# Three input products on unnormalised tiles instead of two, with the first taken out of its bank ahead of the norm's tiles

## The reference, cut to what matters

```python
def rmsnorm(x, g):
    xf = x.astype(jnp.float32)
    y = xf * lax.rsqrt(jnp.mean(xf * xf, axis=-1, keepdims=True) + NORM_EPS)
    return (y * g.astype(jnp.float32)).astype(x.dtype)

for i in range(DEPTH):                      # DEPTH = 2
    h = rmsnorm(x, norm_mix[i])
    proj = h @ w_in[i]
    q, k, v, cb, cc, cx, u, g = jnp.split(proj, IN_SPLITS, axis=-1)
    ...                                     # attention, convolution, state-space scan of u, gates
    x = x + merged @ w_mix_o[i]
    ...                                     # feed-forward
```

## Time and profile before

| | |
|---|---|
| median of three runs | 2523.43 us |
| lowest and highest | 2518.66, 2524.77 us |
| profiled execution | 2524.5 us, of which its span 2522.6 us |

### The profile page before, as it was taken

One profiled execution on the slowest core, in us unless ns is written; L12 is line 12 of the kernel. 1 busy time (PEld: TensorE's weight loads), 2 busy tenths in 40 slices (PEclk: granted clock), 3 DMA queues, 4 the chain that ended last, 5 costly groups with the idle time before them and its releaser, 6 DMA issues.

```text
span 2522.6 us, 33251 instructions
## 1 busy us (share of the span) xinstructions
PE 2433.3 (96%) x12455; PEld 1950.5 (77%) x12455; DVE 1231.0 (49%) x2254; ACT 929.1 (37%) x1470; POOL 1223.1 (48%) x1590
## 2 busy tenths in 40 slices
PE   7899999999999999999999999998988998999999
PEld 5778777888888778877788878887665677788887
DVE  6884653452335668356333143254678844511211
ACT  5233442432322532244242232243436654423322
POOL 3443445555556645354555555564333432555554
PEclk9999999999999999999999999999999999999999
DMA  4222222332222232222233223232310011223232
GB/s 158 85 81 74 91 67 92 108 105 98 96 97 92 93 101 79 82 84 72 88 101 123 96 90 100 88 105 70 115 61 9 1 42 34 100 93 101 93 100 92
DMA packets 81151, 218.06 MB, mean 86 GB/s; under 512 B 15840, under 2 KB 25440, under 8 KB 80608
## 3 DMA queue, kind: packets, MB, share of 16 engines
q1 hardware_dynamic: 61776, 200.43, 24.4%
q10 hardware_dynamic: 19216, 15.51, 2.2%
HBM read 207.26 MB, written 2.10 MB: 83 GB/s over the span
## 4 chain that ended last, share of the span: by engine, by line
PE 84%; DVE 11%; issue 2%; ACT 2%; ACTq 1%; POOL 1%; DMA 0%; DVEq 0%
PE psG L1010 25%; PE psG L1012 25%; PE psG L1011 25%; DVE work_b L2068 1%; PE psT L1189 1%; PE psS L1166 1%; PE psO L1222 1%; DVE tmp L2068 1%; DVE work_m L2068 1%; DVE work_b L2398 1%; PE psS L1097 1%; DVE work_b L2533 1%; ACTq L1717 1%; DVE max L2532 1%; DVE small_work L2068 1%
## 5 line engine op out<-in xcount | busy, mean ns | idle before, releaser
L949 POOL TENSOR_TENSOR w_lo<-w_raw,w_hi 128x256 fp32r<-128x256 f32 x1478 | 1152.0, 810 | 1187.4 <-ACT w_hi L1586 1187.3
L1010 PE MATMUL psG<-h_hi,w_hi 128*128 128x512 f32 x1872 | 747.4, 399 | 12.3 <-POOL w_lo L949 4.1
L1011 PE MATMUL psG<-h_lo,w_hi 128*128 128x512 f32 x1872 | 734.0, 392 | 0.0
L1012 PE MATMUL psG<-h_hi,w_lo 128*128 128x512 f32 x1872 | 733.9, 392 | 0.0
L1586 ACT ACTIVATE w_hi<-w_raw 128x1024 fp32r<-128x1024 f32 (+3 forms) x416 | 402.9, 969 | 501.5 <-PE psG L1012 486.4
L1010 PEld LDWEIGHTS psG<-h_hi,w_hi 128*128 128x128 f32 x1872 | 354.8, 190 | 102.2 <-issue 18.8
L1012 PEld LDWEIGHTS psG<-h_hi,w_lo 128*128 128x128 f32 x1872 | 354.4, 189 | 75.3
L1011 PEld LDWEIGHTS psG<-h_lo,w_hi 128*128 128x128 f32 x1872 | 355.1, 190 | 72.4 <-issue 1.7
L1010 PE MATMUL psG<-m_hi,w_hi 128*128 128x512 f32 x800 | 311.8, 390 | 1.1 <-DVE m_lo L2068 1.1
L1012 PE MATMUL psG<-m_hi,w_lo 128*128 128x512 f32 x800 | 311.4, 389 | 0.0
L1011 PE MATMUL psG<-m_lo,w_hi 128*128 128x512 f32 x800 | 311.4, 389 | 0.0
(11 more groups left out here) (374 smaller groups left out, 2617.4 us busy)
## 6 DMA issues: line engine op xcount, KB each, us to landing
w_raw<-wstream SPq DMA_DIRECT2D x326, 512.0 KB, 3.3
w_raw<-wstream SPq DMA_DIRECT2D x64, 256.0 KB, 2.6
w_raw<-wstream SPq DMA_DIRECT2D x16, 384.0 KB, 3.0
work_b<-work_b ACTq DMA_DIRECT2D x16, 256.0 KB, 3.7
work_b<-cmpw ACTq DMA_DIRECT2D x2, 2048.0 KB, 8.6
x<-xT SPq DMA_DIRECT2D x4, 512.0 KB, 7.1
small_work<-ssmp ACTq DMA_DIRECT2D x8, 256.0 KB, 2.8
outT<-x SPq DMA_DIRECT2D x8, 256.0 KB, 2.0
```

What stands on the lines that cost most here:

```text
L949: ins = pool.tensor_tensor(lo[:, c], w[:, c], hi[:, c].bitcast(F32), ALU.subtract)
L1010: pe.matmul(out, whi, hi, start=(k == 0), stop=False)
L1011: pe.matmul(out, whi, lo, start=False, stop=False)
L1012: ins = pe.matmul(out, wlo, hi, start=False, stop=(k == K - 1))
```

## The change

UNSCALED becomes 3: u0, u1 and u2 run on the tiles without the factor, u3 is the first that reads the norm's. By the same constant, the mean of squares and the spread in layer 0 stand in u2 instead of u1, and `s_read` is counted by u2. VectorE takes u0 out of its bank inside normalise, once the factor is there and ahead of the tiles, since u3 needs this bank; u1 and u2 follow after the tiles. u2 is multiplied out by VectorE and no longer copied by ScalarE.

```diff
-UNSCALED = 2
+UNSCALED = 3
...
                 if name in late:
                     dve.wait_ge(s_rs, late_no[name] + 1)
+                    take_mixer(first_job[name])
                 base = h_norm[name]
...
                 normalise(f"mix{l}", ("norm_mix", l))
-                for i in range(UNSCALED):
+                for i in range(1, UNSCALED):
                     take_mixer(("u", l, i))
```

## The result

| | before | changed |
|---|---|---|
| median, runs on the same chips | 2522.01 us (16 runs, 2517.93 to 2524.77) | 2526.34 us (16 runs, 2521.28 to 2529.22) |
| profiled execution, its span | 2524.5, 2522.6 us | 2527.99, 2526.1 us |

The ratio is 1.0018, 95% interval 1.0011 to 1.0025: 4.3 to 4.5 us slower, between 2.8 and 6.3. That is less than the 0.3% that the prediction took for the least a measurement can tell from no change; the interval is narrower than that and excludes no change. The predicted difference was + 7.4: the time lies in the range and the sign is right, the size is too large.

A forecast was written before the change was run, and what follows sets the result against it. VectorE, not the busy TensorE, was taken to set layer 0's time until 89 us. Layer 0's + 7.7 and layer 1's - 0.3 sum to + 7.4 us, giving 2530.8 us, range 2524.5 to 2535.0.

The forecast's parts named there:

- The mean of squares moves back: Layer 0's norm: the mean moves from u1 to u2, the spread starts 5.4 us late, the norm's tiles 6.1 late.
- Nothing bought on TensorE, q0 waits for its weights: Layer 0: u3 ends at about 46.2 as before; q0 waits for its weights' low part until 48.1, losing 2 us.
- VectorE behind the tiles: Layer 0: u1 and u2 are multiplied out after the tiles, then the coefficients follow, 6.1 us late, at 47.3.
- Contention with GpSimd: Layer 0: GpSimd's weight splits slow 4 more of VectorE's small operations by some 0.5 us each, + 1.9 us.
- The sines absorb nothing: Layer 0: VectorE's 3.01 us pause lies beside ScalarE's sines, so only a 0.4 us margin absorbs delay.
- 7.7 us late is what reaches 88.96 and all that follows: Layer 0's VectorE delay of 7.7 us reaches the scan's first products at 88.96 and everything after in full.
- Rival A: The forecast itself, from + 5.5 us (no added GpSimd contention) to about + 9.5; chance 0.62.
- rival B: VectorE's delay is absorbed; only TensorE's 2.1 us at q0's weights stay: + 1.8 us, 2525.2; chance 0.15.
- Layer 1: Root not delayed; u3's wait for a tile disappears, last tile at about 878.7, a gain of 0.3 us.
- Rival C: TensorE's half-rate clock after its wait ahead of q3 costs 3.6 us; uncovered + 11.0, 2534.4; chance 0.13.
- Rival D: The extra product fills TensorE's wait in layer 0 and the root isn't late: about - 3 us, 2520.4; chance 0.05.
- The last test that the prediction proposed: Prediction is wrong if the distance from 88.96 to the end of the span changes by more than 2 us.

The follow-up runs named there:

- the first experiments: Against the kernel before: the change in layer 0 only, 2527.79 us; the changed kernel with VectorE's scan angles computed before the root, 2527.25 us.
- layer 0 alone: Three unscaled products in layer 0, two in the other layer as in the kernel before: 2527.79 us, ratio 1.0034 against the kernel before.
- in three parts on three products: Changed kernel with the mean of squares in u1 and two thirds of VectorE's scan angles in two earlier pauses: 2520.11 us, ratio 0.9992 against the kernel before.
- the angles ahead of the root: Changed kernel with VectorE computing layer 0's scan angles before the reciprocal, while waiting for the late root: 2527.25 us, ratio 1.0030 against the kernel before.

## Why the prediction was right or wrong, point by point

- **The mean of squares moves back** (predicted: mean at 30.1, reciprocal at 31.4, spread at 33.1, first tile at 35.7): 30.10, 31.48, 33.08, 35.65. Right to 0.1 us, and shown by the kernel that puts it back (27.74, 30.43, no loss).
- **Nothing bought on TensorE, q0 waits for its weights** (u3 from 37.9 to 46.2, q0 at 48.1): 37.94, 46.3 (last start 46.04 + 0.23), 48.05. Right. u3 also ran at half rate at first: its matmuls start 0.43 us apart from 38.50 to 43.62, as u2's did before, and the tiles' pace hid nearly all of it, as the prediction worked out by the Trainium skill's rule ("TensorE: Matmul & The Clock Gate", the HAM clock gate). The last step began 0.35 us after the last low tile was there (45.59 and 45.24; before 0.05), and that lay inside the wait for q0's weights.
- **VectorE behind the tiles**: 6.1 late became 5.7 (45.33 + 1.42 against 39.62 + 1.42), because VectorE waited 1.40 rather than 1.80 us for the last low tile. The first mis-sized term, 0.4 us.
- **Contention with GpSimd**, + 1.9 in the sum: it came as described, and measured 1.4 (the end of the angles went from 55.01 to 62.12, 7.11 late, of which 5.71 were there at the start). The second, 0.5 us. Two parts make it up. The small operations took 2.0 us longer (6.30 and 8.28), as the sum had it. The three operations of 288 columns behind them took 0.6 less (2.36 and 1.80), because GpSimd's next burst lay beside nearly all of them before (47.50 to 49.86, burst from 47.97) and beside the last ones alone now (55.19 to 56.99, burst from 55.74), and the prediction had no term for that. It also counted 19 small operations where the timeline has 17, so its upper bound should be 6 and not 7, and 54.01 + 1.00 + 6.1 + 1.9 is 63.0, not 63.1.
- **The sines absorb nothing**: right. They began at 62.21 and the coefficients at 67.00, 6.8 late; VectorE's pause moved to the other side of the rotation.
- **"7.7 us late is what reaches 88.96 and all that follows"** is the step that failed, in its second half. L1097 is late by 6.94, 5.85 and 5.77 us in the three profiles with layer 0 changed (95.90, 94.81, 94.73). At the first feed-forward's root these kernels stand at 503.94, 501.18 and 500.81, mean 501.98; the three with layer 0 as before (497.96, 498.05, 496.74) at 497.58. The difference is + 4.4 there, and the medians say + 4.3 to + 4.5. So 7.7 were 6.2 at L1097 on average, and 1.8 of these were given back behind it, in work that the change doesn't touch. The profiles scatter by more than that at the root (3.1 us with layer 0 changed, 1.3 without), and the medians on the chip of the first experiments say + 7.8 and + 7.3, so the 1.8 is a best value and not a secured one. Of the 4.5 us by which the forecast of 2530.8 was missed, 1.4 are its start: the three runs had a median of 2523.43, the 16 have 2522.01. Rival A's own lower end was + 5.5, which is 2528.9. The time lies in the stated range because that was stretched to take in rival B, which was wrong as a cause: the hit is in part luck.
- **Where they were given back.** The prediction took TensorE's time behind L1097 as fixed. It isn't: it went with the clock behind the wait ahead of L1097 (L1111, at 98.94 in the kernel before, is the landmark at the end of that stretch). These are windows of 10 us from L1097 on (columns as above), of the kernel before, of the changed kernel's first profile, and of its second:

```profile
89.00:99.00 10.00, 10.00 (x49) 7.91 (x50) 9.26 (x15) 1.02 (x1) 1.18 (x2) 0.83 0.52 131
```

```profile
96.00:106.00 10.00, 10.00 (x44) 7.88 (x44) 9.32 (x15) 1.01 (x1) 1.11 (x2) 0.70 0.49 125
```

```profile
95.00:105.00 10.00, 10.00 (x62) 8.10 (x60) 9.44 (x15) 1.02 (x1) 2.31 (x4) 1.00 0.56 134
```

In the second profile of the changed kernel, TensorE waited only 0.52 us ahead of L1097. VectorE's work for it was done 1.2 us sooner than in the first, and TensorE came 1.1 us later. That lateness was made at q3: behind a wait of 2.80 us for VectorE q3 ran in part at half rate (starts 0.43 us apart from 79.07 to 82.06, granted clock 0.76 from 78 to 85), and took 7.16 us. In the first profile the wait was 1.94, the clock 1.00, and q3 took 5.56 (78.31 to 83.87).

```profile
77.78 0.47 PE L1010 MATMUL psG<-h_hi,w_hi 128*128 128x512 f32 x1 [2.80 <-DVE tmp L2068]
...
84.94 1.02 PE L1291 MATMUL psG<-raw_tile,consts 128*128 128x512 f32 x2
...
94.73 1.92 PE L1097 MATMUL psS<-work_b 128*16 128x128 f32 x16 [0.52 <-DVE work_b L2068]
```

q0 and q1 had run in part at half rate too (12.6 us, 47.95 to 60.56, rather than 11.0), but TensorE was no later for it at q3, which waited for VectorE. Both losses lay beside VectorE's chain and cost nothing; the clock stayed at 1.00 behind L1097, and the stretch from there to L1111 took 8.36 us instead of 9.98 (before) or 11.19 (the changed kernel's first profile). In every profile where that wait was 2.75 to 2.95 us the stretch took 9.7 to 11.2, in every one where it was 0.52 or 2.09 it took 8.3 or 8.4. That is 1.6 of the 2.6 and 2.9 us that the profiles with 0.52 got back between L1097 and the first feed-forward's root (layer 0 alone: from 5.85 to 3.22 late; the changed kernel's second: from 5.77 to 2.85). The changed kernel's first profile lost 1.2 us in this stretch and got 2.2 back behind it (from 6.94 to 5.98 in all), 1.6 of them in the unchanged code from 218 us to the root. That the wait sets the clock behind it fits all eleven profiles, but no run changed the wait alone. That the runs without a profile behave alike is not shown either.
- **Layer 1**: the last low tile at 878.5 in before's time (predicted 878.7), no wait of u3, and locally 0.6 us gained (predicted 0.3). In the medians it can't be seen.
- **Rival B** (VectorE's delay absorbed): refuted as the cause. What ends the wait at L1097 is VectorE, and its delay is there in full. But TensorE's lateness is a second chain behind it: with VectorE's angles out of the way it left L1097 4.3 us late. The size came out between its + 1.8 and A's + 5.5. **Rival C** (half rate ahead of L1097): its condition came, at q3 as it said, in three profiles (the changed kernel's second, layer 0 alone, the mean in u1). q3 took 7.2, 7.2 and 8.4 us instead of 5.5, and the cover held, with 0.52 us of TensorE's wait left in each; its time did not come. The half rate at q0 and q1, in four profiles, was covered in two; with the angles moved (ahead of the root, or in three parts on three products) it lay on the path to the coefficients. At L1097 itself the changed kernel's first profile shows the low level (clock 0.70, 16 matmuls in 3.59 us against 2.70); that is 1.2 us more than before, and one profile. **Rival D**: refuted, the root is late.
- **The last test that the prediction proposed was unfit.** "The distance from 88.96 to the end of the span changes by more than 2 us": it went from 2433.6 to 2430.2. But the kernel before alone shows 2433.6 and 2427.3 in its two profiles. By its own words the prediction is wrong there (3.4 us, where 2 were allowed), and that does point to what was given back, but one profile of each kernel can't show it. The landmark to compare is the nearest one behind the change, over several profiles.

## What to carry to other kernels

Before a product is moved ahead of a reduction's result, look at what else the same constant places: here the mean of squares moved with it and delayed a serial chain over three engines by 5.4 us, and a version without that move lost nothing. The price or gain is read at the engine that sets the next stage (VectorE and the sines, at 49% busy), not at the one with 96%; TensorE won 3.4 us at q0 in one of the experiments and the time did not move. Then ask what stands next in line: with VectorE's chain relieved, TensorE's late q0 held the same stage, and the relief bought nothing. And a sum of local delays doesn't carry to the end unchanged where TensorE's clock goes with the waits on the way (8.36 to 11.19 us for the same stretch here): compare a landmark close behind the change, in more than one profile of each kernel.

## What the hardware showed that I had not expected

**Small VectorE operations go at GpSimd's pace.** Three operations on 128x32 take 0.65 us alone and 2.06 us beside GpSimd's weight splits, that is 0.69 each, and GpSimd's pieces take 8.36 / 12 = 0.70 each. Even operations with one input went from 0.18 to 0.65. These are VectorE and then GpSimd, in the changed kernel:

```profile
48.07 2.06 DVE L2071 SCALAR_TENSOR_TENSOR work_b<-work_b 128x32 f32<-128x32 f32 x3
50.16 0.65 DVE L2075 TENSOR_SCALAR work_b<-work_b 128x32 f32<-128x32 f32 x1
...
53.86 0.18 DVE L2075 TENSOR_SCALAR work_b<-work_b 128x32 f32<-128x32 f32 x1
```

```profile
45.19 8.36 POOL L949 TENSOR_TENSOR w_lo<-w_raw,w_hi 128x256 fp32r<-128x256 f32 x12
```

The slow ones end where GpSimd's burst does, at 53.6. The same preparation of the angles (from the first small operation to the 800-wide ones) took 5.2 us alone (the angles ahead of the root), 8.7 us before and 10.1 us in the changed kernel. The Trainium skill ("SBUF — State Buffer", SBUF: two separate sides) states that the port pair that VectorE and GpSimd share is an exclusive lock, held for a whole instruction. By that rule each small operation waits for one GpSimd piece, and the trace agrees: 0.69 against 0.70 us.

**A wait of 1.6 to 2.8 us may or may not bring the half rate.** Behind the wait for q0's weights, q0 and q1 took 11.0 us in one profile of the changed kernel (wait 1.63) and 12.6 in the other (wait 1.79); in the kernels with the mean in u1 they took 11.0 (waits 1.80 and 1.78) and 12.6 (1.78, with the angles in three parts). The granted clock over the two products was 1.00 where they took 11.0 and 0.86 where they took 12.6. At q3 it is the same: behind waits of 2.79 to 2.81 us it took 7.2, 7.2 and 8.4 us in three profiles (clock 0.76, 0.76, 0.63) and 5.5 in the fourth (clock 1.00, only the first third of the angles moved). The length of the wait alone doesn't decide it, and what does stays open.

**One kernel, two profiles, 6.5 us.** In unchanged code the granted clock was 0.93 in one profile and 0.97 in another, worth 5.2 us over 480. What sets it was not found.
